# Seven block products instead of eight in the gate/up slots of a latent FFN, and the late modulation slots behind its second product

## The reference

```python
FFN_HIDDEN = ((8 * D_MODEL + 3 * 256 - 1) // (3 * 256)) * 256      # 2816 = 11 * 256

def swiglu(u, w_ffn_in, w_ffn_out):
    a, b = jnp.split(u @ w_ffn_in, 2, axis=-1)
    return (jax.nn.silu(a) * b) @ w_ffn_out

for l in range(DEPTH_2):                                            # two layers
    ...
    x = layer_norm(DEEPNORM_ALPHA * x + g1 * (o @ w_out[l]), ln1_g[l], ln1_b[l])
    x = layer_norm(DEEPNORM_ALPHA * x + g2 * swiglu(modulate(x, sh2, sc2), w_ffn_in[l], w_ffn_out[l]), ln2_g[l], ln2_b[l])
```

## Time and profile before

| | |
|---|---|
| median of three runs | 2203.38 us |
| the profiled execution: span from first to last instruction | 2203.0 us (no other time of it is given) |
| TensorE busy | 1987.3 us, 90% |
| VectorE busy | 588.5 us, 27% |
| mean granted TensorE clock | 0.964 of 2.4 GHz |
| L1213: MATMUL rows, busy | 1984 rows, 429.9 us |
| DMA | 664.24 MB, mean 302 GB/s |

### The profile page before, as it was taken

How to read it: one execution, slowest core, us unless ns; L and a number is a source line. 1 busy time by engine, 2 the same in 40 slices (tenths; PEclk the granted TensorE clock), 3 DMA queues, 4 the chain that set the end, 5 groups by cost and what they waited for, 6 DMA issues and landing times.

```text
span 2203.0 us, 32618 instructions
## 1 busy us (share of the span) xinstructions
PE 1987.3 (90%) x14122; PEld 1389.8 (63%) x14122; DVE 588.5 (27%) x1120; ACT 423.4 (19%) x778; POOL 206.2 (9%) x183
## 2 busy tenths in 40 slices
PE   8999899887888888887898887999999999999997
PEld 3857575643455556653565543756888876588886
DVE  6766310124212000000002103353432044640001
...
PEclk9999999999999999999999998999999999999999
...
GB/s 365 372 199 343 339 420 424 417 427 426 421 426 427 423 418 426 420 425 426 421 425 426 416 423 343 140 116 39 222 294 199 180 144 116 1 153 153 129 158 20
DMA packets 181383, 664.24 MB, mean 302 GB/s; under 512 B 17432, under 2 KB 121401, under 8 KB 142649
## 3 DMA queue, kind: packets, MB, share of 16 engines
...
## 4 chain that ended last, share of the span: by engine, by line
PE 58%; DMA 30%; DVE 5%; ACT 4%; issue 1%; POOL 1%; SPq 1%; ACTq 0%; DVEq 0%; POOLq 0%
PE ps L1213 19%; PE ps L692 11%; DMA ring<-in_w_up 8%; DMA ring<-in_w_gate 7%; DMA ring<-in_w_down_slots 7%; DMA ring<-in_context_weights 6%; PE ps L1663 5%; PE ps L1689 2%; PE ps L1048 2%; PE ps L1012 2%; PE ps L1323 2%; DMA arena<-in_w_ada 2%; PE ps L1222 2%; PE ps L1568 1%; ACT arena L2605 1%
## 5 line engine op out<-in xcount | busy, mean ns | idle before, releaser
L1213 PE MATMUL ps<-arena,ring 128*128 128x256 f32 x1984 | 429.9, 379 | 1.0 <-DVEq L392 0.9
L1213 PEld LDWEIGHTS ps<-arena,ring 128*128 128x128 f32 x1984 | 376.5, 190 | 54.2 <-issue 1.7
L1663 PE MATMUL ps<-ring,arena 128*32 128x256 f32 x4000 | 260.5, 407 | 76.2 <-DMA ring<-in_w_up 43.4
L692 PE MATMUL ps<-arena,ring 128*128 128x256 f32 (+1 forms) x1392 | 319.2, 390 | 6.5 <-DMA ring<-in_context_weights 6.5
L692 PEld LDWEIGHTS ps<-arena,ring 128*128 128x128 f32 (+1 forms) x1392 | 256.0, 190 | 76.3 <-DMA ring<-in_context_weights 23.4
L1663 PEld LDWEIGHTS ps<-ring,arena 128*32 128x32 f32 x4000 | 125.4, 115 | 194.9 <-DMA ring<-in_w_up 59.4
L2311 ACT ACTIVATE arena<-ps 128x512 f32<-128x512 f32 (+4 forms) x147 | 78.2, 532 | 739.7 <-PE ps L692 326.8
L1689 PE MATMUL ps<-ring,arena 128*32 128x512 f32 x1024 | 136.9, 660 | 54.4 <-DMA ring<-in_w_down_slots 50.6
L1689 PEld LDWEIGHTS ps<-ring,arena 128*32 128x32 f32 x1024 | 29.0, 114 | 141.1 <-DMA ring<-in_w_down_slots 87.0
L3116 POOL TENSOR_TENSOR XC<-XC,arena 128x256 f32<-128x256 f32 x32 | 23.4, 730 | 986.0 <-ACT XC L2406 965.7
L692 PE MATMUL ps<-ring,arena 128*128 128x256 f32 (+3 forms) x320 | 87.6, 425 | 0.0
...
## 6 DMA issues: line engine op xcount, KB each, us to landing
ring<-in_w_down_slots SPq DMA_DIRECT2D x64, 2048.0 KB, 14.5
ring<-in_w_up SPq DMA_DIRECT2D x63, 2048.0 KB, 13.6
ring<-in_w_gate SPq DMA_DIRECT2D x62, 2048.0 KB, 14.1
ring<-in_w_ada SPq DMA_DIRECT2D x27, 2048.0 KB, 9.6
...
ring<-in_w_in SPq DMA_DIRECT2D x9, 2048.0 KB, 11.6
```

What stands on the lines that cost most here:

```text
L692: m = mm(o, a, x, start=(k == 0 and r == 0), stop=(k == kt - 1 and last))
L1213: m = mm(b, w[:, k, c:c + P], src[:, k, :], start=(k == 0), stop=(k == kt - 1))
L1663: m = mm(b[u][32 * c:32 * c + 32, T * x:T * x + T], xs[:, 2 * h + k, CAP * e:CAP * e + CAP], w[:, k, at_:at_ + T], start=(h == 0 and k == ...
```

## The change

Each of the slots `fi1` to `fi10` becomes a product of 2 x 2 blocks with seven block products in place of eight (Winograd's form of Strassen's scheme). The tokens are cut into two halves of 128, the inputs into two halves of 512, and the columns into gate and up. A block product is four calls: 128 tokens x 128 inputs stay in the array, and 128 inputs x 256 weight columns stream through it; the result lies by token. So the 32 calls become 28.

All sums are on VectorE. Per slot it makes four sums of weight blocks (`weight_sums`, 128 x 1024 each, one slot ahead; T3 in place of the up block B12) and, from the banks, six sums of products: three that open the slot's outputs, one of 128 x 512 that completes the gates and half of the up values, and two more. Per layer it makes four sums of token blocks (128 x 512). ScalarE copies the first product out of its bank and takes SiLU from SBUF. VectorE multiplies into `hid_tok` (by token); TensorE turns it by four transposes into a bank (`hidden_turned`), one slot later, and ScalarE copies that to `HID`. The last slot's turn stands inside the first `fo` slot, behind its twelfth call.

Around this: `weight_sums` for slot 1 stands between `centre` and `normed`; `raw_hidden` is split into `raw_gates`, before the loop, and a rest within slot 1; `carried` stands behind slot 1. The late slots stand behind `fo0` to `fo7` in the stream; `late_slot(m)` stands before `residual(m)`; the first row and turn stand behind `fo3` and `fo4`, the second pair in layer 1 before `rank_and_gate` and behind `forget_gates` (its copy on ScalarE in front of layer 1, its columns on VectorE behind `gate_sums`). The load of the attention bias of layer 1, which lies where the late sums are, moves from before `na_q` to before `nv`. `w_ffn_in` and `w_ffn_out` are laid out by slot in HBM, so that a slot is one transfer with 16 KB or 11 KB in a row per partition. Several semaphores are joined into one, in the same order of events.

```diff
             for j in range(11):
                 stream += part(f"fi{j}")
-                if l == 0 and 0 < j < 9:
-                    stream.append((f"late{j - 1}", ada_slot(I["w_ada_2"][1], j + 3)))
-            stream += part(*[f"fo{m}" for m in range(KD)])
+            for m in range(KD):
+                stream += part(f"fo{m}")
+                if l == 0:
+                    stream.append((f"late{m}", ada_slot(I["w_ada_2"][1], m + 4)))
...
+                def product(o, tokens_, weights, turn=None):
+                    for k in range(4):
+                        if turn is not None:
+                            pe.wait_ge(u_ready[X], KD * (2 * l + 1) + turn + k + 1)
+                        m = mm(o, tokens_[:, k, :], weights[:, k, :], start=(k == 0), stop=(k == 3))
+                    return m
+
+                def hidden_turned(j):
+                    pe.wait_ge(blocks_made, 2 * order(l, j) + 2)
+                    b = open_bank(pe, f"fh{j}_{N}")
+                    for i in range(2):
+                        for t in range(2):
+                            m = tr(b[:, T * i + P * t:T * i + P * t + P], hid_tok[:, t, P * i:P * i + P], ident)
+                    close_bank(m, f"fh{j}_{N}")
+
+                (U11, U12), (U21, U22) = [[U[:, 4 * k:4 * k + 4, P * t:P * t + P] for k in range(2)] for t in range(2)]
+                S1, S2, S3, S4 = tok_sum
                 for j in range(1, 11):
-                    w = take(f"fi{j}{N}")
-                    for x, kind in enumerate(("fa", "fb")):
-                        b = open_bank(pe, f"{kind}{j}_{N}")
-                        tile(b[:, 0:T], w, T * x, U, 2 * l + 1 if j == 1 and x == 0 else None)
-                        close_bank(tile(b[:, T:2 * T], w, T * x + P, U), f"{kind}{j}_{N}")
-                    release_with(f"fb{j}_{N}")
...
-                pe.wait_ge(hj_ready[X], 11 * (l + 1))
+                    only = j == 1
+                    take(f"fi{j}{N}")
+                    (B11, T3), (B21, B22) = weight_blocks(l, j)
+                    T1, T2, T4 = w_sum[j % 2]
+                    b = open_bank(pe, f"f1{j}_{N}")
+                    product(b[:, 0:T], U11, B11, turn=0 if only else None)
+                    b2 = open_bank(pe, f"f2{j}_{N}")
+                    product(b2[:, 0:T], U12, B21, turn=4 if only else None)
+                    pe.wait_ge(sums_made, weights_summed(l, j) - 3)
+                    if only:
+                        pe.wait_ge(sums_made, 44 * l + 5)
+                    close_bank(product(b[:, T:2 * T], S3, T3), f"f1{j}_{N}")
+                    pe.wait_ge(sums_made, weights_summed(l, j) - 2)
+                    if only:
+                        pe.wait_ge(sums_made, 44 * l + 7)
+                    close_bank(product(b2[:, T:2 * T], S2, T2), f"f2{j}_{N}")
+                    if j > 1:
+                        hidden_turned(j - 1)
+                    b = open_bank(pe, f"f3{j}_{N}")
+                    pe.wait_ge(sums_made, weights_summed(l, j) - 1)
+                    product(b[:, T:2 * T], S1, T1)
+                    pe.wait_ge(sums_made, weights_summed(l, j))
+                    close_bank(product(b[:, 0:T], U22, T4), f"f3{j}_{N}")
+                    b = open_bank(pe, f"f4{j}_{N}")
+                    if only:
+                        pe.wait_ge(sums_made, 44 * l + 8)
+                    close_bank(product(b[:, 0:T], S4, B22), f"f4{j}_{N}")
+                    release_with(f"f4{j}_{N}")
+                pe.wait_ge(hj_ready[X], 10 * l + 9)
                 for m_ in range(KD):
                     w = take(f"fo{m_}{N}")
                     b = open_bank(pe, f"fo{m_}_{N}")
-                    close_bank(tile(b[:, 0:T], w, 0, HID, kt=22), f"fo{m_}_{N}")
+                    if m_ == 0:
+                        for k in range(20):
+                            mm(b[:, 0:T], w[:, k, 0:P], HID[:, k, :], start=(k == 0), stop=False)
+                            if k == 11:
+                                hidden_turned(10)
+                        pe.wait_ge(hj_ready[X], 10 * l + 10)
+                        for k in range(20, 22):
+                            m = mm(b[:, 0:T], w[:, k, 0:P], HID[:, k, :], start=False, stop=(k == 21))
+                        close_bank(m, f"fo{m_}_{N}")
+                    else:
+                        close_bank(tile(b[:, 0:T], w, 0, HID, kt=22), f"fo{m_}_{N}")
                     release_with(f"fo{m_}_{N}")
+                    if l == 0:
+                        skip(f"late{m_}")
+                    if l == 0 and m_ == 3:
+                        late_rows(1)
+                    if l == 0 and m_ == 4:
+                        late_turn(1)
...
+                def turned_hidden(j):
+                    evac(f"fh{j}_{N}", HID[:, 2 * j:2 * j + 2, :])
+                    tell(hj_ready[X])
                 for j in range(1, 11):
-                    if j >= 2:
-                        act.wait_ge(hj_ready[X], 11 * l + j - 1)
-                    evac(f"fa{j}_{N}", sga[:, j % 2, :], ACT.Silu)
+                    b = read_bank(act, f"f1{j}_{N}")
+                    step(a(first_copy, b[:, 0:T], ACT.Copy), p1_copied)
+                    if j == 1:
+                        for i in range(2):
+                            act.wait_ge(raw_gate, 2 * l + i + 1)
+                            step(a(rawt[:, i, :], rawt[:, i, :], ACT.Silu, bias=cc[:, i:i + 1]))
+                        tell(sga_ready[X])
+                    else:
+                        turned_hidden(j - 1)
+                    act.wait_ge(blocks_made, 2 * order(l, j) + 1)
+                    step(a(sga[:, j % 2, :].rearrange("p (i t) -> p i t", i=2), blocks[:, 0:2, :], ACT.Silu))
                     tell(sga_ready[X])
-                    if l == 0 and j in (5, 9):
-                        evac(f"late_row{j // 5 + j // 9}", late_row)
+                turned_hidden(10)
+                if l == 0:
+                    evac("late_row1", late_row)
...
+            def weight_sums(l, j):
+                n = fi_slot[l, j]
+                (B11, B12), (B21, B22) = weight_blocks(l, j)
+                T1, T2, T4 = w_sum[j % 2]
+                dve.wait_ge(landed[n % LANES], landing[n])
+                step(tt(B12, B22, B12, ALU.subtract), sums_made)
+                step(tt(T2, B12, B11, ALU.add), sums_made)
+                step(tt(T1, B22, T2, ALU.subtract), sums_made)
+                step(tt(T4, B21, T2, ALU.subtract), sums_made)
...
                 centre(X, l, 0)
+                weight_sums(l, 1)
                 normed(X, l, 0)
-                raw_hidden(l, N)
-                carried(X, l, 0)
+                (U11, U12), (U21, U22) = [[U[:, 4 * k:4 * k + 4, P * t:P * t + P] for k in range(2)] for t in range(2)]
+                S1, S2, S3, S4 = tok_sum
+                dve.wait_ge(u_ready[X], KD * (2 * l + 1) + 4)
+                step(tt(S3, U11, U21, ALU.subtract), sums_made)
+                dve.wait_ge(u_ready[X], KD * (2 * l + 1) + 8)
+                step(tt(S1, U21, U22, ALU.add), sums_made)
+                step(tt(S2, S1, U11, ALU.subtract), sums_made)
+                step(tt(S4, U12, S2, ALU.subtract), sums_made)
+                raw_gates(N)
                 for j in range(1, 11):
+                    n = order(l, j)
+                    dve.wait_ge(p1_copied, n + 1)
+                    b2, b1 = read_bank(dve, f"f2{j}_{N}"), read_bank(dve, f"f1{j}_{N}")
+                    step(tt(with_sixth, first_copy, b2[:, T:2 * T], ALU.add))
+                    step(tt(with_seventh, with_sixth, b1[:, T:2 * T], ALU.add), frees=f"f1{j}_{N}")
+                    step(tt(blocks[:, 0, :], first_copy, b2[:, 0:T], ALU.add), frees=f"f2{j}_{N}")
+                    if j == 1:
+                        raw_hidden(l, N)
+                    if j < 10:
+                        weight_sums(l, j + 1)
+                    b3 = read_bank(dve, f"f3{j}_{N}")
+                    step(tt(blocks[:, 1:4:2, :], bc(with_seventh, 1, 2, T), b3[:].rearrange("p (i t) -> p i t", i=2), ALU.add), blocks_made)
+                    step(tt(with_sixth, with_sixth, b3[:, T:2 * T], ALU.add), frees=f"f3{j}_{N}")
+                    b4 = read_bank(dve, f"f4{j}_{N}")
+                    step(tt(blocks[:, 2, :], with_sixth, b4[:, 0:T], ALU.add), frees=f"f4{j}_{N}")
                     dve.wait_ge(sga_ready[X], 11 * l + j + 1)
-                    b = read_bank(dve, f"fb{j}_{N}")
-                    step(tt(HID[:, 2 * j:2 * j + 2, :], sga[:, j % 2, :].rearrange("p (i t) -> p i t", i=2),
-                            b[:].rearrange("p (i t) -> p i t", i=2), ALU.mult), frees=f"fb{j}_{N}")
-                    tell(hj_ready[X])
...
+                    if j > 1:
+                        read_bank(dve, f"fh{j - 1}_{N}")
+                    step(tt(hid_tok, sga[:, j % 2, :].rearrange("p (i t) -> p i t", i=2), blocks[:, 2:4, :], ALU.mult), blocks_made)
+                    if j == 1:
+                        carried(X, l, 0)
                 if l == 0:
```

(4 more changed lines are left out.)

129 lines of the change are left out of this document (69 added, 60 removed).

## The result

The changed kernel takes 2187.35 us (median of four runs, 2185.97 to 2188.12), the kernel before 2202.1 us beside it. The ratio is 0.9939, 95% interval 0.9924 to 0.9954. The gain is 14.8 us; 24.5 us were forecast, and the time lies inside the range given. On a second chip the same kernel took 2178.86 us against 2200.25 (0.9913, 0.989 to 0.9936). The profiled execution spans 2185.2 us against 2203.0.

What follows compares the result with a forecast made beforehand. TensorE alone was taken to bound the FFN; 34.5 - 10.2 - 2.0 + 1.8 + 0.4 = 24.5 us off 2203.4 gave 2178.9, about 2179 us. The range given was 2172 to 2191.

Steps and rivals of the forecast that it cites:

- Matmuls removed: FFN first product, both layers: 80 calls, 160 rows fewer on TensorE at 0.2159 us each, 34.5 us gained.
- Transposes: FFN slots: 80 added on TensorE at 0.1275 us each, 10.2 us lost; bounds 8.6 and 12.4.
- VectorE's sums: FFN slots in the steady state: 8.8 us of VectorE work hides under TensorE's 12.6 us, cost 0.
- Entry: Start of each FFN: first turn 0.5 us and tight places 0.5 us per layer, 2.0 us lost; bounds 0 and 6.
- Seam: Between first and second FFN product: TensorE's 0.9 us wait per layer for the last product into `HID` goes, gain 1.8 us.
- Late slots: Late slots' moved TensorE work: second row gains 0.99 us, second turn and `late_columns` lose 0.6; net gain 0.4 us.
- transposes at 278 ns: First rival, FFN turns: transposes in fours don't overlap, costing 22.2 us instead of 10.2, time 2191; chance 0.04.
- the `fo` queue: Third rival, layer 0's second product: DMA queue too slow, whole gain gone under 228 GB/s, 2214 at 207 GB/s; chance 0.04.
- VectorE as the bound: Second rival, FFN slots and entries: a 1024-wide sum takes 2.35 us, slot 13.3 us of VectorE work, time 2202; chance 0.03.
- the hand-over: Fourth rival, FFN slots: handing over between four engines makes TensorE wait in every slot, time 2203; chance 0.04.
- the second and fourth rival: VectorE becoming the bound (chance 0.03) and per-slot hand-over waits (chance 0.04), both near no change: 2202 and 2203.

Runs made afterwards that it cites:

- e3: Changed kernel with each of the 80 transposes done twice into the same place: 2186.82 us, 8.0 more than the changed kernel beside it.
- e6: Changed kernel with the last weight sum of slots 3 to 10 made three times: 2187.22 us, 0.9931 of the kernel before.
- e1: Changed kernel with the turn of PSUM banks moved on by four ahead of layer 1's query tiles: 2172.77 us, 0.9879 of the kernel before.
- e4: As e1, with 40 transposes of the first block done twice, moving TensorE's later program on: 2170.94 us, 0.9864 of the kernel before.
- e7: Changed kernel with the last weight sum of slots 3 to 10 made five times: 2211.09 us, 1.0046 of the kernel before.

## Why the prediction was right, and where it was not

The forecast's mechanism held: TensorE alone sets the FFN, and seven products for eight take it down by what the rows cost. The move of the late slots was not run by itself; its parts are read from rows. In the order of the prediction's terms:

- Matmuls removed, 34.5 us. Right: a slot's 56 rows take 12.09 us, 0.2159 each.
- Transposes, 10.2 us. 8.8: 0.11 each (e3), near the lower bound of half a row. The eight from which I took 0.1275 were a piece of the chain, which runs to the end of the last record. In the timeline of the kernel before, the product behind them starts 0.93 us after the first of them, 0.116 each; read so, the row would have given 9.3 us:

```profile
1925.80 1.09 PE L1155 MATMUL ps<-tab,arena 128*128 128x128 f32 x8
1926.73 2.32 PE L1125 MATMUL ps<-arena,ring 128*128 128x256 f32 x10
```

- VectorE's sums, 0. Right in the steady state: 1.22 us as read off the line through the narrower rows, and 3.80 us of idle time a slot where 3.8 were forecast. VectorE was busy for 71% of the ten slots instead of 65%. e6 shows the place with least room to be the second slot's turn (0.77 us), not every slot's 3.6.
- Entry, 2.0 us. 1.1: the first turn's 0.67 and 0.45 us as forecast; the tight places ahead of it held without a wait, where 0.5 each had been allowed.
- Seam, gain 1.8. Right (0.90 and 0.91 gone).
- Late slots, net gain 0.4, bounds -0.4 and 1.0. This is the step that failed. Its parts: the gain of 0.99 us by the second row came, the row standing where TensorE waited for `modulate`; there is 0.17 us of wait left of 1.16. The DMA was right: `fo` in layer 0 took 78.5 us (1686.73 to 1765.23) without a wait, at 353 GB/s in its last seven steps. The second turn and its column sum cost 1.36 us instead of 0.6: 0.81 for the turn in full, since TensorE had 0.14 us of waiting behind its projections and not the 0.4 that I counted (from the first level's 48 rows to the next product 1.21 us before, 1.07 now), and 0.55 for the second projection, held by the bank that `late_columns` frees behind `gate_sums`. I looked at what `late_columns` delays on VectorE, not at the bank that it keeps.
- Not in the sum at all: 3.06 us of bank waits at L743 and `wo` (e1), and 1.97 us of stop (e4). The order that I compared was that of the instructions on each engine. It was the same for these rows before and after; what had changed was the bank behind the same line, by a count of tiles two stages earlier. The remaining 0.17 us of the mixer stay unexplained.

The FFN came out 2.5 us better than its terms (27.6 for 25.1 with the late row), and the mixer 6.0 us worse (6.6 lost for 0.6). So behind the first border the profiled execution gained 21.1 us instead of 24.5. The first block takes 3.3 us of this back in the first pair of profiles, which leaves the 17.8 between their spans; over all profiles the first stretch ran from 1528 to 1544 us in the changed family and from 1530 to 1541 in that of the kernel before, and why it varies stays open. The other 3.0 us down to the measured 14.8 lie between these two executions and the medians, and no trace shows them. The changed kernel's own medians on two chips, 2187.35 and 2178.86 us, lie on both sides of what the stretches give (2203.4 less 21.1, 2182.3). So the range was met partly because two errors of opposite sign offset each other, and that the second median equals the forecast of 2178.9 is luck: in that chip's profile the mixer lost 10.2 us, and the first stretch was 9.4 us shorter than in the first profile of the kernel before.

The rivals: transposes at 278 ns fell by e3, the `fo` queue by 353 GB/s and the absence of a wait; VectorE as the bound and the hand-over became real only with 2.5 and 5 us more work a slot (e6, e7). In the prediction's chances the second and fourth rival add up to 0.07, where it has 0.06; nothing hangs on it.

The Trainium skill ("TensorE: Matmul & The Clock Gate", Part 4: PE-mode transpose) has about 275 ns for a transpose in a kernel's context. The record's length agrees with it (273 ns, the median of 80); as a price in a row of four it is two and a half times too high: 0.109 us by e3.
